# Six chunks of the modulation summed by VectorE instead of TensorE, and their weights spread over more of the projections

## What is computed

```python
def adaln(cond, w_mod, b_mod):                       # cond is c for x, c_ctx for ctx
    m = jax.nn.silu(cond) @ w_mod + b_mod            # 1024 -> 3 x 1024
    return _split(m, (D_MODEL, D_MODEL, D_MODEL))    # shift, scale, gate

h_lat = rms_norm(x_lat, g_pre[layer]) * (1 + sc_l[:, None]) + sh_l[:, None]
xv, g_hy, q, k, v, g_att = _split(h @ w_in, EVEN_SPLITS)
x_lat = x_lat + ga_l[:, None] * rms_norm(y_lat, g_post[layer])
```

## Time and profile before

| | us |
|---|---|
| median of 3 runs | 1784.21 (1783.65 to 1784.56) |
| span of the profiled execution | 1780.9 |
| PE busy in it | 1732.2 |
| DVE busy in it | 1164.9 |
| first product of the stage's projections | 51.53 |
| last product of the stage | 185.81 |
| first product of the next stage | 186.72 |

### The profile page before, as it was taken

How to read it: one execution, slowest core, us unless ns; L and a number is a source line. 1 busy time by engine, 2 the same in 40 slices (tenths; PEclk the granted TensorE clock), 3 DMA queues, 4 the chain that set the end, 5 groups by cost and what they waited for, 6 DMA issues and landing times. The chain is left out here.

```text
span 1780.9 us, 22805 instructions
## 1 busy us (share of the span) xinstructions
PE 1732.2 (97%) x8527; PEld 1394.0 (78%) x8527; DVE 1164.9 (65%) x2141; ACT 914.3 (51%) x1490; POOL 49.4 (3%) x68
## 2 busy tenths in 40 slices
PE   8999999999998999999999999999999999999998
PEld 3776788777787877777777787788887787878886
DVE  6653466698437557767866775777646867577744
ACT  4333444333336356655656556467534756547743
POOL 0000000000000000000100002000000002000000
PEclk9999999999999999999999999999999999999999
DMA  9466211121425444443544444555554454555562
GB/s 333 155 200 226 95 56 64 54 70 67 142 95 175 132 125 146 147 139 107 180 147 153 147 154 155 176 177 193 198 189 157 127 175 134 183 165 183 189 218 76
DMA packets 115972, 267.23 MB, mean 150 GB/s; under 512 B 5412, under 2 KB 9837, under 8 KB 115672
## 3 DMA queue, kind: packets, MB, share of 16 engines
q1 hardware_dynamic: 111384, 252.26, 43.3%
q0 software_dynamic: 3504, 10.96, 2.0%
q10 hardware_dynamic: 976, 2.57, 0.4%
HBM read 264.63 MB, written 1.14 MB: 149 GB/s over the span
## 5 line engine op out<-in xcount | busy, mean ns | idle before, releaser
L146 DVE TENSOR_TENSOR qw_rest<-weights,qw_lead 128x1024 fp32r<-128x1024 f32 (+2 forms) x428 | 520.1, 1222 | 380.5 <-ACT qw_lead L334 375.3
L334 ACT ACTIVATE qw_lead<-weights 128x1024 fp32r<-128x1024 f32 (+2 forms) x428 | 446.4, 1048 | 461.5 <-PE psum L173 421.6
L173 PE MATMUL psum<-qw_lead,b_h_pair 128*128 128x512 f32 (+1 forms) x960 | 319.9, 398 | 3.3 <-ACT b_gates L2927 1.4
L173 PEld LDWEIGHTS psum<-qw_lead,b_h_pair 128*128 128x128 f32 x960 | 180.4, 188 | 43.8 <-issue 3.7
L173 PE MATMUL psum<-qw_rest,b_h_pair 128*128 128x512 f32 (+1 forms) x480 | 186.2, 388 | 0.0
L166 PE MATMUL psum<-b_h_pair,qw_lead 128*128 128x512 f32 x512 | 178.1, 392 | 2.0 <-DVE b_h_pair L713 2.0
L167 PE MATMUL psum<-b_h_pair,qw_rest 128*128 128x256 f32 x512 | 143.3, 280 | 0.0
L173 PE MATMUL psum<-e_h_lead,qw_lead 128*128 128x512 f32 x320 | 141.0, 441 | 1.8 <-DVE e_qT L1532 1.4
L173 PE MATMUL psum<-e_h_lead,qw_rest 128*128 128x512 f32 x320 | 125.7, 393 | 0.0
L173 PE MATMUL psum<-e_h_rest,qw_lead 128*128 128x512 f32 x320 | 124.9, 390 | 0.0
L166 PEld LDWEIGHTS psum<-b_h_pair,qw_lead 128*128 128x128 f32 x512 | 95.8, 187 | 23.7 <-DVE b_h_pair L713 2.9
(11 more groups left out here) (481 smaller groups left out, 3011.9 us busy)
## 6 DMA issues: line engine op xcount, KB each, us to landing
weights<-in_w_in SPq DMA_DIRECT2D x48, 1024.0 KB, 5.1
weights<-in_o_w_in SPq DMA_DIRECT2D x32, 1024.0 KB, 5.4
weights<-in_w_mlp_up SPq DMA_DIRECT2D x32, 1024.0 KB, 5.5
weights<-in_w_mlp_down SPq DMA_DIRECT2D x32, 1024.0 KB, 4.9
weights<-in_e_w_in SPq DMA_DIRECT2D x26, 1024.0 KB, 5.1
weights<-in_w_mod SPq DMA_DIRECT2D x24, 1024.0 KB, 7.1
weights<-in_e_w_out SPq DMA_DIRECT2D x8, 1024.0 KB, 4.9
weights<-in_o_w_out SPq DMA_DIRECT2D x8, 1024.0 KB, 4.9
```

The lines of the kernel that those rows point to most:

```text
L146: return eng.tensor_tensor(self.rest[at], src, self.lead[at].bitcast(F32), ALU.subtract)
L173: mm = nc.tensor.matmul(out, l, r, start=start and i == 0, stop=stop and i == 2)
L334: self.core.nc.scalar.activation(self.buf.lead[self.at(u)], self.raw(u), ACT.Copy).then_inc(self.lead_ready, 1)
```

## The change

The six chunks of mods1 are now done by a new class, `SideMods`. For each half, DVE multiplies the four 128 x 512 slices by the value of `cond` for their row and adds them into an accumulator of 128 x 512, once for main and once for ctx: 8 operations for each half, 16 for each chunk, of which the first two only scale (`tensor_scalar`) and the others scale and add (`scalar_tensor_tensor`). There are two pairs of accumulators. At the end of a chunk PE transposes both (8 products) and DVE reduces 128 x 8 x 128 columns as before. The copies by ACT fall away. The halves of the modulation now lie beside quarters 3, 4, 6, 7, 9, 10, 12, 13, 15, 16, 18 and 19 (`slots`), and a half is free when its 8 operations are done. `late` is gone. One `silu` of e_gatt waits for the fifth turn, since its target held an accumulator.

```diff
+MODS1 = ((0, 4), (0, 5), (1, 0), (1, 1), (1, 2), (1, 3))
...
-    cols("e_q2", w, (EV_Q + 512,), chunks=chunks)
-    cols("e_gatt", w, (EV_GATT, EV_GATT + 512), chunks=chunks)
+    cols("e_kv", w, (EV_KV,), beside=(3,))
+    cols("e_q", w, (EV_Q,), beside=(0, 2, 3))
+    cols("e_q2", w, (EV_Q + 512,), beside=(1, 2))
+    cols("e_gatt", w, (EV_GATT, EV_GATT + 512), beside=(0, 1, 3, 4, 6, 7))
...
             if h + w.RAW < len(w.halves):
-                sp.wait_ge(sem, value)
+                if isinstance(sem, Mods):
+                    sem.wait_used(sp, value)
+                else:
+                    sp.wait_ge(sem, value)
                 w.load(sp, h + w.RAW)
...
+class SideMods(Mods):
...
+    def wait_used(self, sp, n):
+        for sem in self.added:
+            sp.wait_ge(sem, 4 * n + 4)
...
+            for c in range(4):
+                yield self.at[n] + 0.45 * c + 0.2 * s
...
+                if r + c == 0:
+                    ins = eng.tensor_scalar(acc, z, weight, None, ALU.mult)
+                else:
+                    eng.wait_ge(added, 4 * n + c)
+                    ins = eng.scalar_tensor_tensor(out=acc, in0=z, scalar=weight, in1=acc, op0=ALU.mult, op1=ALU.add)
+                ins.then_inc(added, 1)
...
+            for s in range(2):
+                pe.wait_ge(self.added[s], 8 * i + 8)
+                for b in range(4):
+                    mm = nc.tensor.transpose(ps[:, self.pair[s], b * P:(b + 1) * P], self.accs[i % 2][s][:, b * P:(b + 1) * P], self.core.ident[:])
+            mm.then_inc(self.spread, 1)
...
-    mods1 = Mods(core, "m1_", r, [(0, 4), (0, 5), (1, 0), (1, 1), (1, 2), (1, 3)], raws, [15.9 + 2 * n for n in range(12)],
-                 (r.rows2,), (4,), (5,), second_free, lambda pe: None)
+    slots = (3, 4, 6, 7, 9, 10, 12, 13, 15, 16, 18, 19)
+    mods1 = SideMods(core, "m1_", r, MODS1, first["mod1"], [2.0 * n for n in slots],
+                     ((core.hT[:, 6, :], core.hT[:, 7, :]), (r.rows2, core.ga[:, 2, BANK:2 * BANK])), (4, 5), accs_free, second_free,
+                     [2.0 * slots[2 * i + 1] + 3.3 for i in range(len(MODS1))], by_vector=(0, 1))
...
-    feed = Feed(core, (dense,), (mods0, mods1), prime=(-4.4, -4.3, -2.0), late=(first["e_q2"], 1.75), defer=True)
+    feed = Feed(core, (dense,), (mods0, mods1), prime=(-4.4, -4.3, -2.0), defer=True)
```

More of the change, by code:

```diff
@@ L189, in mods, with cols @@
                 mod_half(l, j, r)
-    def cols(name, w, starts, width=BANK, chunks=None):
+    def cols(name, w, starts, width=BANK, beside=()):
         first[name] = len(units)
-        for s in starts:
+        for i, s in enumerate(starts):
             for r in range(w.shape[0] // BANK):
@@ L196, in cols @@
                 halves.append([(w[r * BANK:(r + 1) * BANK, s:s + width].rearrange("(k p) n -> p k n", p=P), 0, 4, width)])
-                chunk = chunks.pop(0) if chunks else None
                 for q in range(2):
-                    if chunk:
-                        mod_half(*chunk, q)
+                    if 4 * i + 2 * r + q in beside:
+                        first["mod1"].append(len(units))
+                        mod_half(*chunks.pop(0))
                     units.append((at, q * 2 * width, 2, width, True))
@@ L211, in weight_stream @@
     w = a["e_w_in"][0]
-    cols("e_kv", w, (EV_KV,))
-    chunks = [(0, 4), (0, 5), (1, 0), (1, 1), (1, 2), (1, 3)]
-    cols("e_q", w, (EV_Q,))
-    cols("e_q2", w, (EV_Q + 512,), chunks=chunks)
-    cols("e_gatt", w, (EV_GATT, EV_GATT + 512), chunks=chunks)
+    chunks = [(l, j, r) for l, j in MODS1 for r in range(2)]
+    first["mod1"] = []
+    cols("e_kv", w, (EV_KV,), beside=(3,))
+    cols("e_q", w, (EV_Q,), beside=(0, 2, 3))
+    cols("e_q2", w, (EV_Q + 512,), beside=(1, 2))
+    cols("e_gatt", w, (EV_GATT, EV_GATT + 512), beside=(0, 1, 3, 4, 6, 7))
     cols("e_x1", w, (1024, 1536))
@@ L291, in __init__, with quarters @@
         self.buf = Split(core.nc, core.ctx, "qw", [P, self.BUF, 1024])
+    def quarters(self, name, n):
+        u = self.first[name]
+        return [v for v in self.split_units if v >= u][:n]
     def uses(self, u, steps):
@@ L1957, in kv_dve, with silu, out @@
         return out if g % 2 else None
[L1958 to L1965, removed]
+    items = [Item(**span(stream.quarters("e_kv", 4), 0.0, 2.0), groups=tokens(BANK), src=r.h, act=kv_act, dve=kv_dve, ready_k=enter.wait_ready)]
+    items.append(Item(**span(stream.quarters("e_q", 4), 8.0, 2.0), groups=tokens(BANK), src=r.h, **heads_out(0)))
+    items.append(Item(**span(stream.quarters("e_q2", 4), 16.0, 2.0), groups=tokens(BANK), src=r.h, **heads_out(BANK)))
+    def silu(k):
+        def out(act, src):
+            if k == 6:
+                act.wait_ge(mods1.spread, mods1.spread_at(4))
+            return nc.scalar.activation(core.hT[:, k, :], src, ACT.Silu)
+        return out
     for i in range(2):
-        items.append(Item(**span(range(u + 8 * i + 1, u + 8 * i + 8, 2), 24.0 + 8 * i, 2.0), groups=feats, src=r.h,
+        items.append(Item(**span(stream.quarters("e_gatt", 8)[4 * i:4 * i + 4], 24.0 + 8 * i, 2.0), groups=feats, src=r.h,
                           act=lambda g, i=i: silu(4 * i + g)))
```

58 lines of the change are left out of this document (53 added, 5 removed).

## The result

The changed kernel took 1828.89 us (median of four runs, 1826.83 to 1830.8), the kernel before 1784.38 beside it (1783.65 to 1785.55). The ratio is 1.0248, 95% interval 1.0234 to 1.0262: slower by 44.5 us. The forecast was 1820, slower, with a range of 1798 to 1838. The profiled execution of the changed kernel took 1826.8 us, its span is 1825.0.

The account below looks back on a forecast made before the run. PE bounded the stage before; DVE would become the bound. 71.2 start + 116.4 work + 32.8 waits + 2.9 tail = 223.3 against 186.7, +36.6, taken as +36 on 1784.2: 1820 us, range 1798 to 1838.

Parts of the forecast that it names:

- The step on which it rested: In the changed stage, DVE repeatedly waits for loads that its own additions have only then released; 32.8 us idle in all.
- The walk: Engine queues followed with trace durations through q8 to q20, giving six DVE waits of 3.8 to 6.8 us.
- the ring: DVE's last addition releases a projection load, ACT's cast waits for it, DVE waits for the cast: 32.8 us; chance 0.70.
- The price of an addition: Each of DVE's 84 scaled additions of 128 x 512 taken at 0.67 us, from the earlier trace.
- rival 4: DVE's additions with two float32 inputs in SBUF run at half the pace: 50 us more, 1870; chance 0.03.
- PE's stalls: From q8 on PE waits 10, 5.7, 7 and 10 us; the same delay as DVE's, not added to its sum.
- the tail: After the last addition: eight transposes 0.8, reduction, shift and scale 1.2, step to the next stage 0.9; 2.9 us.
- the sum: Next stage's first product at 71.2 + 116.4 + 32.8 + 2.9 = 223.3 us, against 186.7: +36.6.
- rival 1: Same waits plus PE's slow pace, so casts for q15 to q19 wait for PE too: +44 to +52, 1832; chance 0.10.
- rival 2: DVE bounds the stage, but load landings hide behind its other work: +3.8 us, 1788; chance 0.12.
- rival 3: DVE's 59.4 us idle time absorbs the additions if they cost at most about 0.5 us: -10, 1774; chance 0.05.
- the two errors named for it: Downward errors: additions at 0.60 us, 6 us less; each of six waits 2 us shorter, 12 less; 18 with both.

## Why the prediction was right

**The step on which it rested held.** The walk gave the six places at which DVE stands and how long. The trace after:

```profile
93.81 1.23 DVE L146 TENSOR_TENSOR qw_rest<-weights,qw_lead 128x1024 fp32r<-128x1024 f32 x1 [5.30 <-ACT qw_lead L343]
110.42 1.23 DVE L146 TENSOR_TENSOR qw_rest<-weights,qw_lead 128x1024 fp32r<-128x1024 f32 x1 [4.89 <-ACT qw_lead L343]
153.08 1.23 DVE L146 TENSOR_TENSOR qw_rest<-weights,qw_lead 128x1024 fp32r<-128x1024 f32 x1 [6.27 <-ACT qw_lead L343]
172.25 1.22 DVE L146 TENSOR_TENSOR qw_rest<-weights,qw_lead 128x1024 fp32r<-128x1024 f32 x1 [3.79 <-ACT qw_lead L343]
190.21 1.23 DVE L146 TENSOR_TENSOR qw_rest<-weights,qw_lead 128x1024 fp32r<-128x1024 f32 x1 [5.55 <-ACT qw_lead L343]
211.95 1.23 DVE L146 TENSOR_TENSOR qw_rest<-weights,qw_lead 128x1024 fp32r<-128x1024 f32 x1 [6.23 <-ACT qw_lead L343]
```

| quarter | q8 | q10 | q14 | q16 | q18 | q20 | sum |
|---|---|---|---|---|---|---|---|
| walked | 4.7 | 5.0 | 6.3 | 3.8 | 6.8 | 6.2 | 32.8 |
| measured | 5.30 | 4.89 | 6.27 | 3.79 | 5.55 | 6.23 | 32.0 |

Six waits of ACT for loads of `in_e_w_in`, as said. The waits agree better than the times at which they come: the walk is 2 us early at q14's load (144.7 against 146.89) and 7 at q20's (199 against 205.80). A single wait doesn't feel this, since it counts from its own release. The experiments show more than the sum of these rows: the ring costs 34.4 us.

**The price of an addition held.** Additions start 0.66 us apart (104.13 and 104.79 above), where 0.67 was taken; the group's row (ns of one) gives nearly the length of the earlier trace rows:

```profile
L1213 DVE SCALAR_TENSOR_TENSOR x_res<-weights,cond,x_res x21: 737/744/749, 100.2 to 224.9; 128x512 f32<-128x512 f32 x21
```

With that rival 4 is out: 84 additions with a float32 weight and a float32 sum, both in SBUF, took 0.74 us for 512 columns, not the length of an operation on 1024. That the trace does not agree with the Trainium skill ("Vector Engine (DVE) Microarchitecture Reference", section "Points that are easy to get wrong"), as the prediction has it, says too much. The sentence there says that the throughput of this form is halved, but not from which pace. Against the scaling, which has the same shape and one tensor input, the addition is indeed slower: 0.66 us from start to start against 0.39 (98.23 and 98.62), 1.7 times. The rows speak only against a doubled price beside an operation with two tensor inputs. The sum took its price from the rows and lost nothing by this.

**PE's stalls held in place, less so in size.** The places walked were q8 (10 us), the gates' second turn (5.7), q12 (7) and q14's turn (10). PE's idle times of over 2.4 us in the changed kernel were 10.89 at 111.02, 7.02 at 129.44 (the gates' turn, line 1233 now), 4.33 at 153.68, 2.45 at 165.16, 5.32 at 180.67, 3.15 at 192.87, and the two at the end:

```profile
225.81 1.03 PE L1227 MATMUL psum<-ident,x_res 128*128 128x128 f32 x4 [4.02 <-DVE x_res L1213]
226.64 1.06 PE L1227 MATMUL psum<-ident,ga 128*128 128x128 f32 x4
230.10 1.19 PE L1531 MATMUL psum<-e_qT 128*128 128x512 f32 x1 [2.40 <-PEq L120]
```

The delay came in more and smaller stalls from q12 on, and a part of it as a slower pace. In the main these are DVE's delay seen from PE, as the prediction said, and DVE's last addition (225.59) sets the end.

**The step that was mis-sized: what else came to DVE.** The first product of the next stage starts at 230.10, not at 223.3. The working priced twelve scalings and 84 additions and counted a single reduction, in the tail, at the price of small operations; that all six now read 1024 columns instead of 32 follows from the changed kernel's `parts`, and the price of a long reduction over PSUM could have been bounded from rows: the kernel before has `128x1<-128x512` in 0.69 us. The missing term is 6.2 us, worth 5.7 when taken out alone.

That it is nearly the 6.8 us is in part luck, since smaller errors offset each other. The tail's 1.2 us of reduction and scale operations are in the sum twice: the last chunk's were done by DVE at 183.48 to 184.5 in the kernel before, inside the 38.84 us of the earlier trace rows. From 71.18 to 230.10 DVE was busy for 120.0 us, where the sum has 117.6 with that: 2.4 more, though the reductions bring 6.2. It was idle for 38.9, where the sum has 34.5: 4.4 more. The largest idle time outside of the six waits is 2.33 us at 199.13, for a turn of heads on PE, which the walk did not have; 1.02 and 0.69 are the rotary sums' turns. The tail, from the end of the last addition (225.59 + 0.66) to 230.10, was 3.8 us instead of 2.9: the turns took 0.83 and 1.06 at PE's slow pace, the reduction 1.22.

**The sum against the medians.** The start of the next stage moved by 43.4 us (186.72 to 230.10) and the medians by 44.5, so nothing but this shift is to be explained, within 1.1 us. The forecast fell 8.5 us short of the median's shift (36 against 44.5): 6.8 by the start of the next stage, 0.6 by rounding the sum down, 1.1 outside.

**What the working didn't see.** It said that the wait for a cast holds back a copy in ACT's queue and that the stalls "don't add to DVE's sum". True of the changed kernel, but it hides how much hung on that order: with the copies first, 30 of the ring's 34 us are gone at the new places. At the new places the copies-first order gives DVE work between the release of a load and its `qw_rest`; at the old places the same order still paid 26.6, and why it finds no such work there was not traced. What is shown is that neither the spread alone (34.4 left) nor the order alone (26.6 left) cures the ring, and both together do (4.2 left).

**The rivals.** The slow pace of PE (rival 1) would have been 1832; the measured 1828.9 lies between it and the 1820. Of the excess 5.7 us went with the wide reductions. PE's pace was not tested apart; DVE's one long wait for PE inside the stage is the 2.33 us above. DVE without a ring (rival 2, 1788) was made by taking the halves out of the ring: 1794.5, that is 6.5 more than worked out, about the size of the reductions. The idle time of DVE as cover (rival 3) falls: with no half in the ring all six chunks still cost 10 us, and two chunks gained nothing. Its threshold takes the 12.3 us off the additions (60.3), where it is the idle time (59.4) that shrinks; that gives 47 us over 96 additions in place of 48, still 0.5 each. The range, too, was laid a little wide: its lower end of 1798 is 22 us below the forecast, and the two errors named for it come to 18.

## What to carry to other kernels

Work moved to an idle engine can cost more than its sum, as here, when that engine's last use of a buffer releases a load that the same engine waits for a few instructions later: walk the ring (last use, load, landing, cast, next use) with the landing time of this kernel before counting idle time as free. Price every operation that the new code issues, also the one at the end that turns the result, at its new width. And test placement and engine apart: here the placement alone cost nothing and the order of copies and casts alone cost nothing, but with the sums on DVE each was worth some 30 us (1831.2 and 1828.9 against 1800.2). Last, don't take an engine's waits for their cost: 43 us of DVE's waits for casts cost nothing where PE set the time, and 44 us went with a loss of 34 where the casts waited for loads that DVE itself held back.

## What the runs showed of the hardware

- A reduction of 1024 PSUM columns to 8 sums took 1.22 us on DVE, one of 32 columns 0.19.
- PE's granted clock fell behind the long stall and stayed below 1.00 for the 40 us from 100 on. The windows of the changed kernel by 10 us:

```profile
90.00:100.00 10.00, 10.00 (x45) 8.07 (x43) 6.15 (x11) 2.01 (x2) 0.00 (x0) 1.00 0.46 173
100.00:110.00 10.00, 0.12 (x1) 0.00 (x0) 5.54 (x9) 0.67 (x1) 0.00 (x0) 0.65 0.31 105
110.00:120.00 10.00, 8.61 (x30) 6.31 (x31) 9.51 (x12) 2.88 (x5) 0.00 (x0) 0.67 0.12 25
120.00:130.00 10.00, 2.98 (x14) 2.12 (x13) 8.08 (x16) 3.11 (x6) 0.00 (x0) 0.85 0.49 186
130.00:140.00 10.00, 10.00 (x42) 8.24 (x41) 9.93 (x20) 1.81 (x3) 1.59 (x3) 0.81 0.36 107
```

It is a mean of the two levels, 1.2 and 2.4 GHz. Behind the 10.89 us of idle time a product started every 0.43 us (111.58, 112.01, 112.44), before it every 0.23 (99.28, 99.51, 99.74). What it cost was not measured apart. DVE set the time, and its one long wait for PE in the stage was 2.33 us.
- The second of two loads issued 0.42 us apart (181.26 and 181.68) let its cast start 7.4 us after its issue (189.12), a single one 5.1 us.
